# Sharing the first weight split among three engines, and taking the decay row sums from two f32r products: one change to a 512-token hybrid block on one core

## The reference, cut to what matters

```python
h = rms_norm(x, norm_mix_w)                  # x * rsqrt(mean(x*x) + 1e-6) * w
proj = h @ w_in
qkv_a = silu(causal_depthwise_conv(qkv_a, conv_w))
log_decay = -exp(a_log) * softplus(alpha_a + dt_bias)      # g, per token and head
G = cumsum(g, axis=-1)                                     # inside a chunk
decay = exp(where(causal, G[..., :, None] - G[..., None, :], -inf))
a_mat = where(strict, beta * (k k^T) * decay, 0) + I
qk = where(causal, (q k^T) * decay, 0)
```

## Time and profile before

| | |
|---|---|
| median of three runs | 653.88 us (653.12 to 654.07) |
| the profiled execution | 654.05 us, of which the span in the trace is 652.3 us |
| granted TensorE clock over the span | 0.992 |
| TensorE busy | 629.6 us (97%) |
| VectorE busy | 481.5 us (74%) |
| ScalarE busy | 393.5 us (60%) |
| GpSimd busy | 172.6 us (26%) |

### The profile page before, as it was taken

The page is one execution under the profiler, slowest core; times in us unless marked ns, Lnnn a source line. Parts: engine busy times, 40 slices in busy tenths (PEclk is TensorE's granted clock), DMA queues, the critical chain, the costliest instruction groups (busy, mean ns, idle before and its releaser), DMA issues.

```text
span 652.3 us, 9545 instructions
## 1 busy us (share of the span) xinstructions
PE 629.6 (97%) x3492; PEld 511.8 (78%) x3493; DVE 481.5 (74%) x816; ACT 393.5 (60%) x680; POOL 172.6 (26%) x216
## 2 busy tenths in 40 slices
PE   7999999899999999999999997999999999999984
PEld 6788878777778878888888875788888888888763
DVE  5878995698523443534764688899999999998877
ACT  7538585446625333234532562688988998898743
POOL 7000005998000000000000001154745645546200
PEclk9999999999999999999999998999999999999998
DMA  8656543122621222134136944367778787975573
GB/s 263 196 160 207 149 81 110 53 65 67 150 84 50 65 83 82 29 87 107 65 130 238 359 176 154 102 203 264 247 263 273 220 296 232 314 263 164 200 279 129
DMA packets 76961, 108.53 MB, mean 166 GB/s; under 512 B 31863, under 2 KB 54464, under 8 KB 76786
## 3 DMA queue, kind: packets, MB, share of 16 engines
q1 hardware_dynamic: 64320, 99.76, 47.5%
q0 software_dynamic: 12480, 8.11, 4.2%
q10 hardware_dynamic: 114, 0.04, 0.0%
HBM read 123.90 MB, written 20.98 MB: 222 GB/s over the span
## 4 chain that ended last, share of the span: by engine, by line
PE 86%; DVE 7%; POOL 2%; DMA 2%; issue 1%; ACT 1%; SPq 0%; POOLq 0%; DVEq 0%; ACTq 0%
PE bank L1799 23%; PE bank L1801 22%; PE bank L1800 22%; PE bank L2274 3%; PE bank L1865 1%; DMA expert_rows<-expert_rows_hbm 1%; DVE rank_onehot L1637 1%; PE bank L1987 1%; PE bank L2011 1%; PE bank L1997 1%; DVE w_lo L1176 1%; PE bank L2290 1%; PE bank L2050 1%; PE bank L2174 1%; PE bank L1853 1%
## 5 line engine op out<-in xcount | busy, mean ns | idle before, releaser
L1799 PE MATMUL bank<-h_hi,w_hi 128*128 128x512 f32 x288 | 118.3, 411 | 0.0
L1801 PE MATMUL bank<-h_hi,w_lo 128*128 128x512 f32 x288 | 112.6, 391 | 0.0
L1800 PE MATMUL bank<-h_lo,w_hi 128*128 128x512 f32 x288 | 112.3, 390 | 0.0
L1511 DVE TENSOR_TENSOR gate_up_lo<-ew_raw,gate_up_hi 128x1024 fp32r<-128x1024 f32 x92 | 108.4, 1219 | 3.4 <-PE bank L1801 2.0
L1176 DVE TENSOR_TENSOR w_lo<-w_raw,w_hi 128x2048 fp32r<-128x2048 f32 x26 | 59.9, 2305 | 46.6 <-ACT w_hi L838 46.5
L770 POOL DMA_INDIRECT unit_tokens<-ffn_rows,row_index x23 | 27.7, 1206 | 249.5 <-DVE row_index L1645 238.8
L1053 ACT ACTIVATE gate_up_hi<-ew_raw 128x1024 fp32r<-128x1024 f32 x92 | 92.0, 1053 | 0.0
L1799 PE MATMUL bank<-gate_up_hi,unit_in_hi 128*128 128x512 f32 x184 | 75.8, 412 | 0.6 <-DVE unit_in_lo L1671 0.6
L1801 PE MATMUL bank<-gate_up_hi,unit_in_lo 128*128 128x512 f32 x184 | 72.2, 392 | 0.0
L1800 PE MATMUL bank<-gate_up_lo,unit_in_hi 128*128 128x512 f32 x184 | 71.8, 390 | 0.0
L1799 PEld LDWEIGHTS bank<-h_hi,w_hi 128*128 128x128 f32 x288 | 54.1, 188 | 13.2 <-issue 2.2
(11 more groups left out here) (409 smaller groups left out, 1284.8 us busy)
## 6 DMA issues: line engine op xcount, KB each, us to landing
w_raw<-in_w_in SPq DMA_DIRECT2D x16, 1024.0 KB, 5.8
ew_raw<-in_w_gate SPq DMA_DIRECT2D x32, 512.0 KB
ew_raw<-in_w_up SPq DMA_DIRECT2D x32, 512.0 KB
ew_raw<-in_w_down SPq DMA_DIRECT2D x32, 512.0 KB
expert_rows_hbm<-sub_product SPq DMA_DIRECT2D x16, 256.0 KB
w_raw<-in_w_out SPq DMA_DIRECT2D x4, 1024.0 KB, 5.0
expert_rows<-expert_rows_hbm SPq DMA_DIRECT2D x8, 512.0 KB, 7.3
x_T<-in_x SPq DMA_DIRECT2D x4, 512.0 KB, 5.5
```

Source lines behind the costliest of these rows:

```text
L1511: dve.tensor_tensor(dst, eraw[slot][:, :], hi.bitcast(F32), ALU.subtract).then_inc(elo_done, 1)
L1799: pe.matmul(out_ap, lhs_hi, rhs_hi, start=first, stop=False)
L1800: pe.matmul(out_ap, lhs_hi, rhs_lo, start=False, stop=False)
L1801: return pe.matmul(out_ap, lhs_lo, rhs_hi, start=False, stop=last)
```

## The change

1. The last tile of x is loaded in two transfers. VectorE squares and sums its first half (`half_mean`, divided by 1024 with epsilon added), ScalarE squares the second half and takes the root with `half_mean` as its bias.
2. The first 128 columns of weights are loaded in two transfers. ScalarE and VectorE make hi and lo of the first half, GpSimd both of the second half, after some of its fills; the other fills move behind.
3. In item 0 the product with `h_lo` of k follows the two hi products of k+1.
4. `gdt` is split into a high and a low part by two more VectorE operations. GpSimd makes the sources of the row sums of both parts, eight products of `tri` with a broadcast; the four of VectorE fall away.
5. Each row sum is two f32r products into one bank in place of one f32 product.

```diff
+        src_hi = [at(f"row_source_hi{i}", [P, HA, P], F32R, o) for i, o in enumerate((r_o + 8256, r_o + 10304, r_tmp, r_tmp + 2048))]
+        src_lo = [at(f"row_source_lo{i}", [P, HA, P], F32R, r_b + 2048 * i) for i in range(TT)]
@@ sync
-            for t in range(TT):
+            for t in range(TT - 1):
                 sp.dma_start(x[:, t, :], a["x"][0, t * P:(t + 1) * P, :]).then_inc(x_in[t], 16)
+            sp.dma_start(x[:, TT - 1, 0:S], a["x"][0, S - P:, 0:S]).then_inc(x_in[TT - 1], 16)
+            sp.dma_start(x[:, TT - 1, S:], a["x"][0, S - P:, S:]).then_inc(last_half_in, 16)
...
-                        sp.dma_start(dst[:, :, 0:P], src[:, :, 0:P]).then_inc(first_in, 16)
+                        for i in range(2):
+                            ks = slice(KT // 2 * i, KT // 2 * (i + 1))
+                            sp.dma_start(dst[:, ks, 0:P], src[:, ks, 0:P]).then_inc(first_in[i], 16)
@@ gpsimd
+            nc.gpsimd.iota(no_row[:, :], pattern=[[0, 1]], base=int(EMPTY), channel_multiplier=0).then_inc(no_row_set, 1)
+            nc.gpsimd.memset(sub_t[:, :, :], 0.0).then_inc(pool_set, 1)
+            pool.wait_ge(first_in[1], 16)
+            link(nc.gpsimd.tensor_copy(kv_(whi[0])[:, KT // 2:, 0:P], kv_(raw[0])[:, KT // 2:, 0:P]))
+            pool.wait_ge(pool_set, ZERO_SET)
+            nc.gpsimd.tensor_tensor(kv_(wlo[0])[:, KT // 2:, 0:P], kv_(raw[0])[:, KT // 2:, 0:P],
+                                    kv_(whi[0])[:, KT // 2:, 0:P].bitcast(F32), ALU.subtract).then_inc(pool_set, 1)
...
+            pool.wait_ge(gates_done, 2)
+            for t in range(TT):
+                for dst, part in ((src_hi, gdt_hi[:, t, :].bitcast(F32)), (src_lo, gdt_lo[:, t, :])):
+                    ins = nc.gpsimd.tensor_tensor(dst[t][:, :, :], bc_mid(tri[:, :], HA), bc_last(part, P), ALU.mult)
+                ins.then_inc(rb_ready, 1)
@@ scalar
+            act.wait_ge(last_half_in, 16)
+            link(act.activation(junk[:, 0:S], x[:, TT - 1, S:], ACT.Square, accum_out=ssq[:, TT - 1:TT]))
+            act.wait_ge(cols_done, HALF_MEAN)
+            act.activation(rst[:, TT - 1:TT], ssq[:, TT - 1:TT], ACT.Sqrt, scale=1.0 / D, bias=half_mean[:, :]).then_inc(ssq_done, 1)
+
+            act.wait_ge(first_in[0], 16)
+            act.activation(kv_(whi[0])[:, 0:KT // 2, 0:P], kv_(raw[0])[:, 0:KT // 2, 0:P], ACT.Copy).then_inc(hi_done, 1)
@@ vector
+                    dve.wait_ge(x_in[TT - 1], 16)
+                    link(dve.scalar_tensor_tensor(x_square[:, :], x[:, TT - 1, 0:S], 1.0, x[:, TT - 1, 0:S], ALU.mult, ALU.mult,
+                                                  accum_out=half_mean[:, :]))
+                    dve.tensor_scalar(half_mean[:, :], half_mean[:, :], 1.0 / D, EPS, ALU.mult, ALU.add).then_inc(cols_done, 1)
...
-                if k == 2:
-                    dve.wait_ge(hi_done, 1)
-                    dve.tensor_tensor(kv_(wlo[0])[:, KT // 2:, 0:P], kv_(raw[0])[:, KT // 2:, 0:P],
-                                      kv_(whi[0])[:, KT // 2:, 0:P].bitcast(F32), ALU.subtract).then_inc(lo_done, 1)
...
-                    ins.then_inc(gates_done, 1)
+                    link(ins)
+                    link(dve.tensor_copy(gdt_hi[:, :, :], gdt[:, :, :]))
+                    dve.tensor_tensor(gdt_lo[:, :, :], gdt[:, :, :], gdt_hi[:, :, :].bitcast(F32), ALU.subtract).then_inc(gates_done, 1)
...
-                    for t in range(TT):
-                        row_source(t)
@@ tensor
-                pe.matmul(ps[2 + t % 2][:, :], ones[:, :], front[t][:, :, :], start=True, stop=True).then_inc(row_ps, 1)
+                ones_r = ones[:, :].bitcast(F32R)
+                pe.matmul(ps[2 + t % 2][:, :], ones_r, src_hi[t][:, :, :], start=True, stop=False)
+                pe.matmul(ps[2 + t % 2][:, :], ones_r, src_lo[t][:, :, :], start=False, stop=True).then_inc(row_ps, 1)
...
-                        pe.wait_ge(ht_lo, k + 1)
-                        ins = pe.matmul(bank[:, :], wh, h_lo[:, k, :], start=False, stop=k == KT - 1)
+                        for j in (k - 1, k) if k == KT - 1 else range(max(0, k - 1), k):
+                            if j:
+                                pe.wait_ge(ht_lo, j + 1)
+                            ins = pe.matmul(bank[:, :], hi[:, j, 0:P], h_lo[:, j, :], start=False, stop=j == KT - 1)
```

More of the change, by code:

```diff
@@ L146, in build @@
         junk = at("square_junk", [P, D], F32, r_tmp)
+        x_square = at("x_square_half", [P, S], F32, r_o)
         rows = at("small_rows", [65, P], F32, r_tmp + 4096)
@@ L268, in build @@
         warm = new("root_of_eps", [P, 1])
+        half_mean = new("mean_square_half", [P, 1])
         rsq_i = new("rsqrt_seed", [P, TT * HA], mybir.dt.int32)
@@ L273, in build @@
         gdt = new("log_decay_T", [P, TT, HA])
+        gdt_hi, gdt_lo = new("log_decay_hi", [P, TT, HA], F32R), new("log_decay_lo", [P, TT, HA])
         alog = new("a_log_b", [P, HA])
@@ L319, in build @@
         x_in = [sem(f"x_in{t}") for t in range(TT)]
+        last_half_in = sem("x_last_second_half_in")
         small_in = sem("small_in")
@@ L379, in build @@
         pool_set = sem("gpsimd_set")
-        IDENT_SET, CONSTS, DIST_SET, ROUTE_CONSTS, ZERO_SET, SUB_DONE = range(1, 7)
+        IDENT_SET, CONSTS, DIST_SET, ZERO_SET, FIRST_ROWS_LO, ROUTE_CONSTS, SUB_DONE = range(1, 8)
         no_row_set, nothing_in = sem("index_past_all_rows_set"), sem("first_indirect_moved_nothing")
@@ L390, in build @@
         late_hi, late_lo = sem("late_out_hi_done"), sem("late_out_lo_done")
-        first_in, first_hi = sem("w_first_rows_in"), sem("w_first_rows_hi")
-        half_done = sem("dve_half_done")
-        FIRST_ROWS_LO = 1
+        first_in = [sem(f"w_first_rows_in{i}") for i in range(2)]
+        SMALL_COLS, HALF_MEAN = 1, 2
         w_in = a["w_in"][0].rearrange("(k p) n -> p k n", p=P)
@@ L605, in _ @@
                     sp.wait_ge(lo_done, split_count(u - RING))
+                    if u == RING:
+                        sp.wait_ge(pool_set, FIRST_ROWS_LO)
                 for dst, src in unit_sources(u):
                     if u == 0:
-                        sp.dma_start(dst[:, :, 0:P], src[:, :, 0:P]).then_inc(first_in, 16)
+                        for i in range(2):
+                            ks = slice(KT // 2 * i, KT // 2 * (i + 1))
+                            sp.dma_start(dst[:, ks, 0:P], src[:, ks, 0:P]).then_inc(first_in[i], 16)
                         dst, src = dst[:, :, P:], src[:, :, P:]
@@ L742, in _ @@
             nc.gpsimd.iota(row_i[:, :], pattern=[[1, P]], base=-255, channel_multiplier=0).then_inc(pool_set, 1)
-            nc.gpsimd.iota(no_row[:, :], pattern=[[0, 1]], base=int(EMPTY), channel_multiplier=0).then_inc(no_row_set, 1)
-            nc.gpsimd.memset(sub_t[:, :, :], 0.0).then_inc(pool_set, 1)
             link(nc.gpsimd.memset(sub_x[:, :, :], 0.0))
@@ L1196, in _ @@
                         dve.tensor_scalar(x_, x_, rst[:, t:t + 1], None, ALU.mult).then_inc(x_scaled, 1)
-            dve.wait_ge(first_hi, 1)
+            dve.wait_ge(hi_done, 1)
             dve.tensor_tensor(kv_(wlo[0])[:, 0:KT // 2, 0:P], kv_(raw[0])[:, 0:KT // 2, 0:P],
-                              kv_(whi[0])[:, 0:KT // 2, 0:P].bitcast(F32), ALU.subtract).then_inc(half_done, 1)
-            dve.wait_ge(cols_done, 1)
+                              kv_(whi[0])[:, 0:KT // 2, 0:P].bitcast(F32), ALU.subtract).then_inc(lo_done, 1)
             for k in range(KT):
-                if k == 2:
-                    dve.wait_ge(hi_done, 1)
-                    dve.tensor_tensor(kv_(wlo[0])[:, KT // 2:, 0:P], kv_(raw[0])[:, KT // 2:, 0:P],
-                                      kv_(whi[0])[:, KT // 2:, 0:P].bitcast(F32), ALU.subtract).then_inc(lo_done, 1)
                 dve.wait_ge(ht_hi, k + 1)
@@ L1245, in rsqrt @@
                     link(dve.scalar_tensor_tensor(y, t, 1.5, y, ALU.add, ALU.mult))
-            def row_source(t):
-                dve.tensor_tensor(front[t][:, :, :], bc_mid(tri[:, :], HA), bc_last(gdt[:, t, :], P), ALU.mult).then_inc(rb_ready, 1)
             def decay_args(t):
@@ L1877, in _ @@
                 else:
-                    pe.wait_ge(hi_done, 1)
-                    pe.wait_ge(half_done, FIRST_ROWS_LO)
+                    pe.wait_ge(lo_done, 1)
                     pe.wait_ge(pool_set, CONSTS)
@@ L1887, in _ @@
                             pe.wait_ge(ht_lo, 1)
-                        elif k == KT // 2:
-                            pe.wait_ge(lo_done, 1)
+                        if k == KT // 2:
+                            pe.wait_ge(pool_set, FIRST_ROWS_LO)
                         pe.wait_ge(ht_hi, k + 1)
```

## The result

The changed kernel took 656.64 us (median of 8; 655.83 to 658.25), the kernel before 653.81 beside it: ratio 1.0044, 95% interval 1.0033 to 1.0055. It is slower by 2.8 us. The profiled execution took 656.53 us with a span of 654.7, 2.48 us more than before's. The one change made two opposite ones: the start gained about 1 us, the decay stage lost 3.4.

What follows compares the result with a forecast made beforehand. TensorE and VectorE were taken as near their limit in the decay stage, with the decay chain arriving last. 654.05 − 0.35 + 4.9 = 658.6, less 0.17 to the median: 658.4 us; range 654.0 to 661.5.

Steps and rivals of the forecast that it cites:

- second rival: Decay stage: some waits of VectorE for GpSimd are hidden, five of eight bite: +2.3, 656.0 us; chance 10%.
- The start, −0.35: First product of TensorE: with halved loads of x and weights it starts at 13.85 instead of 14.22 us: −0.35 us.
- The bound of +0.75: Start: its slow limit, if GpSimd's subtraction gets in before VectorE's w_lo: +0.75 us.
- Row sums, −1.6 on TensorE, worth 0: TensorE, decay stage: four f32 products become four f32r pairs, 1.6 us less, but it waits that much longer: 0.
- The relief of 2.07, worth 0: VectorE, decay stage: 2.07 us net less work is worth 0, since k_decayed's fourth operation needs ScalarE's last square sum.
- Multiply-adds wait as the product of two SBUF tiles does: conv(5) and conv(6): VectorE's multiply-adds wait for GpSimd like a TENSOR_TENSOR with two SBUF inputs, 1.3 to 1.8 us instead of 0.75.
- third rival: Decay stage: multiply-adds do not wait for GpSimd; the decay chain shifts by 0.42 alone: 654.1 us, no change; chance 16%.
- The hold, 0.87 us net each: Decay stage: each of GpSimd's eight operations holds VectorE for its length less 0.14 us: 0.97, counted as 0.87 net.
- the decay chain's +4.9: Decay chain on VectorE and ScalarE: k_decayed starts at 68.4 instead of 63.48, eight waits of 0.87 less 2.07: +4.9 us.
- Rival 1: Decay stage: GpSimd keeps its turn through its eight unlinked operations, VectorE gets none in between: +6.5, 660.2 us; chance 10%.
- The two holes: TensorE, decay stage: idle before the third row sum (4.4 us) and before the turns of q (1.65 us).
- The claim that the clock costs 0: TensorE behind the 4.4 us hole: half speed for 3 us loses 1.5 us, inside the turns' 1.65 wait: 0.

Runs made afterwards that it cites:

- experiment 5: The changed start with no sources: each row sum is four f32 products per tile, broadcast log decay as stationary side; 654.48 us, ratio 1.0010.
- the ninth run: The eighth plus a separate bank and early arguments for tile 0, f32r pairs for tiles 1 to 3 with later GpSimd sources; 653.90 us, ratio 0.9992.
- experiment 6: The changed kernel with 13 more products ahead of the third row sum, so that TensorE is not idle there; 657.25 us, ratio 1.0055.
- run 2: The start of the kernel before with the changed decay stage; 657.04 us, ratio 1.0055.
- the first run: The changed start with the decay stage of the kernel before; 652.10 us, ratio 0.9987.
- the tenth: The kernel of the first run again, beside the ordered start on one chip; 652.72 us, ratio 0.9986 to the kernel before.
- seventh: The kernel of experiment 5 with a bank of its own for tile 0 and its arguments made before conv(7); 654.18 us, ratio 1.0006.
- third run: The changed kernel with four f32 sources on GpSimd in place of eight halves, and f32 row sums; 653.64 us, ratio 1.0003.
- eighth: The changed start alone, with GpSimd's half of the first weights held until VectorE's low part is made; 653.44 us, ratio 0.9993.
- eleventh: The kernel of the eighth again, beside the start alone on one chip; 652.91 us, ratio 0.9992.
- the fourth: The changed kernel with all eight sources made by VectorE ahead of conv(6), none by GpSimd; 654.47 us, ratio 1.0022.

## Why the prediction was right and where its sizes were off

The direction was right and 656.64 lies in the range, 1.8 us under the forecast. It lies below the 657.2 to 660.9 that the prediction gave to its own mechanism, in a stretch that it left to the second rival, although the mechanism is the forecast's. Start and decay were missed in the same direction, by 0.7 and 1.5 us, so neither hid the other. By its steps:

- **The start, −0.35.** Measured −1.06 in the profile, −0.9 us in the runs of the half alone (0.9987 and 0.9986 of 653). The charge of 0.5 us for sharing was about right (0.42); what was mis-sized is what lies ahead of it. The half of x was squared from 8.36, where I had taken 8.75 (the profiles with this start have 8.31 to 9.03, so the changed kernel's had some luck), and from there to the first product it took 4.80 us instead of 5.1. The bound of +0.75 exists; it is the last section's subject.
- **Row sums, −1.6 on TensorE, worth 0.** Right: the products stand 0.23 us apart, and the time came back as idle time.
- **The relief of 2.07, worth 0.** Right by the distance in experiment 5 (41.56 against 41.51); its time does not show it.
- **Multiply-adds wait as the product of two SBUF tiles does.** Right: 1.42 us apart instead of 0.75. This was the step that decided the sign (third rival), and no row of before showed it. The Trainium skill, "SBUF — State Buffer", section Who interferes with whom, says that a VectorE instruction with two SBUF inputs contends with a GpSimd instruction that reads SBUF; by that rule the multiply-adds wait, and the trace agrees (1.42 us). Of instructions with one SBUF input the section says that only those in a two-port mode contend, and counts `tensor_scalar` among the ones that can enter it: here a scaling waited in the changed kernel (1.33 us for 0.48), and k_decayed, whose other input is in PSUM, did not in the ninth run (2.68 us beside GpSimd).
- **The hold, 0.87 us net each.** This is the term of the sum that was mis-sized. I took GpSimd's whole length less 0.14 us, from one wait in the earlier trace rows; that gives 0.97, and the sum went on with 0.87 without saying why. The number of waits and their order were as played through, but they measured 5.5 us, 0.69 each. With both engines queued, a multiply-add (0.75) and a source (1.00 from start to start) together take 1.45 us and not 1.75, so 0.3 us of the two pass side by side; which part of an operation that is, no run shows. The difference of 8 × 0.18 = 1.4 us is nearly all by which the decay chain's +4.9 was too much: k_decayed began 3.55 us later, the turns of q 3.38.
- **Rival 1 (GpSimd keeps its turn): wrong.** Unlinked GpSimd operations alternate with VectorE's too: beside the multiply-adds of conv(5), 1.42 us apart, GpSimd's start 1.45 us apart.
- **Rival 2 (five of eight bite, 656.0).** Nearest in time and wrong in mechanism: all eight bite.
- **The two holes.** The first was sized 4.4 us and is 3.12, as the chain is less late. The second, 1.65 us at the turns, was not seen: the low clock took its place. The claim that the clock costs 0 is borne out for the changed kernel's profile (experiment 6), and is not general (run 2).

What is open: the stretch behind the turns differs by 3 us between two profiled executions of one kernel (the start alone: 650.2 − 93.26 = 556.9 us in the first run, 653.1 − 93.16 = 559.9 in the tenth). That is more than any gain ahead of the turns, so single profiles show the distances but not the totals. The traces of these two do show where most of it arises. From the chain that ended last, near the end of the program, two lines of the first run, then the same two of the tenth:

```profile
622.21 6.69 DMA expert_rows<-expert_rows_hbm
...
632.97 1.72 PE bank L2363 x4
```

```profile
622.38 7.78 DMA expert_rows<-expert_rows_hbm
...
634.75 2.86 PE bank L2363 x4
```

The last transfer of rows took 1.09 us longer, TensorE waited 1.92 us there instead of 0.83, and behind that wait its clock was low: four passes took 2.86 us and not 1.72. Why this transfer varies is open. Open too is why the fifth and seventh kernels are 1.2 to 1.5 us slower than the start alone.

## What to carry to other kernels

Before work is handed to GpSimd, look at what VectorE runs beside it: where VectorE has two inputs in SBUF, and in the scalings here with one, it took turns with GpSimd's products, and a GpSimd operation can hold VectorE for longer than VectorE would need to do it (0.69 against 0.60 us here). Beside operations that read PSUM, as in the ninth run, it cost nothing. And where two chains end within 0.2 us of each other, relief of one alone gave 0 and 0.15 us here; how close they are can be read from the trace before anything is built.

## What was not expected of the hardware

**The start has two outcomes.** From VectorE's square of x's half (which begins when x's half has arrived and VectorE is free) to the first product it took 4.79 to 4.84 us in nine profiles and 5.73 and 5.72 in the third and fifth. In those two GpSimd's cast began before 10.6 us, got in between VectorE's two scalings (1.28 us instead of 0.88), and its subtraction then got in before VectorE's low part:

```profile
10.16 1.28 DVE L1221 TENSOR_SCALAR x_T<-x_T,rms_factor 128x512 f32<-128x512 f32 x2
10.55 0.61 POOL L749 CAST w_hi<-w_raw 128x512 fp32r<-128x512 f32 x1 [1.03 <-DMA w_raw<-in_w_in]
11.25 1.32 POOL L751 TENSOR_TENSOR w_lo<-w_raw,w_hi 128x512 fp32r<-128x512 f32 x1
11.36 1.76 DVE L1223 TENSOR_TENSOR w_lo<-w_raw,w_hi 128x512 fp32r<-128x512 f32 x1
14.04 0.57 PE L1914 MATMUL bank<-h_hi,w_hi 128*128 128x512 f32 x1 [1.89 <-DVE h_lo L1227]
```

Weights that land 0.35 us earlier (10.55 against 10.90) thus make the first product 0.9 us later. And the longer idle time can cost the clock as well. In the third run's profile TensorE was idle for 1.89 us before its first product, and the two microseconds behind it were:

```profile
14.00:16.00 2.00, 1.96 (x5) 1.59 (x6) 2.00 (x4) 2.00 (x5) 1.31 (x13) 0.57 0.71 107
```

Its products stood 0.43 us apart until 17.4, and the log decay came 40.06 us after the first product. In the fifth run's profile, after the same 1.89 us, the clock stayed at 1.00 and it came after 38.43. So the slow start cost 0.9 us in one execution and 2.5 in the other; that may be most of the 2.95 us by which the third run's profiled execution (656.59) is above its median. With the order fixed (eighth, ninth and eleventh) it was 4.79 or 4.80, but in none of these did the weights come early, so that it cures the slow outcome is argued and not shown.

**The low clock behind a hole lasted differently**: after 3.12 us of idle time products stood 0.43 us apart until 86.1 (3 us), after 3.08 us in the second run until 89.7 (5.7 us), and after 2.34 us in the fourth the clock fell only near 84, 1 us after TensorE had resumed. An idle time of 1.9 us was followed by it in two profiles (the third run's start, the tenth run's end) and not in the fifth run's start.
